# 44 slots of the first tile's expert mixer moved among the attention heads of the last tiles

## The reference

```python
def peer(h, w_pq, keys, u_tab, v_tab):
    ...
        q = (hb @ w_pq).reshape(t, P_HEADS, 2, P_QDIM // 2)
        sc = jnp.einsum('thpd,hpkd->thpk', q, keys).astype(jnp.float32)
        sv, si = lax.top_k(sc, P_TOPK)
        ...
        cv, ci = lax.top_k(cand, P_TOPK)
        eidx = jnp.take_along_axis(cidx, ci, axis=-1)
        gate = jax.nn.softmax(cv, axis=-1)
        act = jax.nn.gelu(jnp.einsum('thkd,td->thk', u_tab[eidx], hb).astype(jnp.float32))
        return jnp.einsum('thk,thkd->td', (gate * act).astype(hb.dtype), v_tab[eidx])
```

## Time and profile before

| | us |
|---|---|
| median of 3 runs | 5101.31 (5096.21 to 5101.77) |
| the profiled execution: its own time | 5101.03 |
| its span, first to last instruction | 5099.2 |
| PE busy | 3987.9 (78%) |
| DVE busy | 2904.9 (57%) |
| ACT busy | 1637.7 (32%) |
| DMA moved | 1577.22 MB, mean 309 GB/s |

### The profile page before, as it was taken

The page is one execution under the profiler, slowest core; times in us unless marked ns, Lnnn a source line. Parts: engine busy times, 40 slices in busy tenths (PEclk is TensorE's granted clock), DMA queues, the critical chain, the costliest instruction groups (busy, mean ns, idle before and its releaser), DMA issues.

```text
span 5099.2 us, 61250 instructions
## 1 busy us (share of the span) xinstructions
PE 3987.9 (78%) x19854; PEld 1568.1 (31%) x19854; DVE 2904.9 (57%) x6339; ACT 1637.7 (32%) x4803; POOL 1522.9 (30%) x1453
## 2 busy tenths in 40 slices
PE   5989988998886666666679899889988756666666
PEld 3555564232321111111134556633323211111111
DVE  3541464666787666554445414546667876665544
ACT  0222143333333333333322211433333333333333
POOL 0210002333444444333312100023333344443332
PEclk7989999999986777666679899999998867677666
DMA  7113305999999999999951133069999999999998
GB/s 280 48 51 124 132 26 210 408 413 383 421 415 393 421 421 421 421 421 421 421 195 48 51 128 136 18 239 407 411 396 421 394 399 421 421 421 421 421 421 355
DMA packets 223883, 1577.22 MB, mean 309 GB/s; under 512 B 25744, under 2 KB 27984, under 8 KB 35920
## 3 DMA queue, kind: packets, MB, share of 16 engines
q0 software_dynamic: 184320, 1342.26, 63.9%
q1 hardware_dynamic: 39248, 231.06, 12.1%
HBM read 1569.94 MB, written 3.28 MB: 309 GB/s over the span
## 4 chain that ended last, share of the span: by engine, by line
PE 40%; DMA 35%; DVE 16%; issue 4%; ACT 3%; DVEq 2%; SPq 0%; POOL 0%; ACTq 0%; POOLq 0%
DMA arena<-in_experts,arena 28%; PE ps L759 14%; PE ps L993 8%; DVE sq L1471 7%; DMA front<-in_experts,arena 6%; PE ps L944 4%; PE ps L969 3%; PE ps L896 2%; PE ps L957 2%; PE ps L921 2%; PE ps L908 1%; DMA arena<-in_weights 1%; DVE negm L1365 1%; DVE arena L1197 1%; PE ps L825 1%
## 5 line engine op out<-in xcount | busy, mean ns | idle before, releaser
L993 PE MATMUL ps<-arena 64*64 64x512 f32 x9088 | 1645.1, 810 | 834.4 <-ACT arena L1134 788.3
L732 POOL DMA_INDIRECT arena<-in_experts,arena x1136 | 1228.6, 1081 | 2824.6 <-PE ps L993 1738.0
L1471 DVE CUSTOM_DVE_ANT_0 sq<-arena 128x1024 f32<-128x1024 f32 x1136 | 1393.2, 1226 | 990.2 <-DMA arena<-in_experts,arena 926.5
L993 PEld LDWEIGHTS ps<-arena 64*64 64x64 f32 x9088 | 326.3, 162 | 2040.9 <-issue 2012.8
L1128 ACT ACTIVATE arena<-arena 128x1 f32<-128x1 f32 x1280 | 259.2, 203 | 1978.7 <-DVE arena L1471 1977.9
L759 PE MATMUL ps<-arena 128*128 128x512 f32 (+3 forms) x1920 | 787.7, 558 | 1.9 <-ACT arena L1042 0.9
L1134 ACT ACTIVATE arena<-ident,arena 128x128 f32<-128x128 f32 x1280 | 513.9, 401 | 91.6 <-issue 3.3
L759 PEld LDWEIGHTS ps<-arena 128*128 128x128 f32 x1920 | 353.2, 190 | 416.1 <-issue 377.7
L1130 ACT ACTIVATE arena<-arena 128x1 f32<-128x1 f32 x1280 | 376.8, 294 | 92.4 <-issue 5.6
L969 PE MATMUL ps<-arena 128*128 128x256 f32 (+1 forms) x1024 | 331.3, 466 | 3.1 <-issue 2.3
L993 PE MATMUL ps<-front,arena 64*64 64x512 f32 x1152 | 200.1, 770 | 90.2 <-ACT arena L1134 90.1
(11 more groups left out here) (158 smaller groups left out, 3005.7 us busy)
## 6 DMA issues: line engine op xcount, KB each, us to landing
arena<-in_weights SPq DMA_DIRECT2D x182, 1024.0 KB, 7.4
arena<-in_experts,arena POOLq DMA_INDIRECT x1136, 21.5
arena<-mod_rows SPq DMA_DIRECT2D x30, 512.0 KB, 6.9
arena<-in_weights SPq DMA_DIRECT2D x8, 576.0 KB, 4.6
arena<-in_keysT SPq DMA_DIRECT2D x4, 1024.0 KB, 9.8
arena<-in_weights SPq DMA_DIRECT2D x4, 768.0 KB, 4.2
arena<-in_weights SPq DMA_DIRECT2D x6, 512.0 KB, 3.5
front<-in_experts,arena POOLq DMA_INDIRECT x144, 15.2
```

What stands on the lines that cost most here:

```text
L732: pool.indirect_dma_start(out=ring[BUF[n]], out_offset=None, in_=ins["experts"], in_offset=bass.IndirectOffsetOnAxis(ap=index(t)[:, slot:s ...
L993: last = MM(acc[h][to:to + 64, c * 512:(c + 1) * 512], diag[n % 4][lo:lo + 64, lo:lo + 64], ring[BUF[n]][lo:lo + 64, D + c * 512:D + (c + ...
L1471: V.tensor_tensor_reduce(out=sq[:], in0=ring[BUF[n]][:, 0:D], in1=h2_of_slot(n), scale=1.0, scalar=0.0, op0=ALU.mult, op1=ALU.add, accum_o ...
```

## The change

Slots 0 to 43 of tile 0 (`FRONT` = 44) stand among the last 28 heads of tiles 2 to 4 in place of behind them, in both layers. To make room:

- all 26 items of `choose(l, 0)` stand among the first 20 heads (`mixed`), not among 48;
- the front slots use four buffers in turn: 4, and the new 11, 12 and 13. Buffer 11 is a gap gained by moving `va(0)`, `vc(0)` and others; 12 and 13 are two of the three weight blocks, so the loads that filled them early (`gate` half 2 and `proj` of the merge of tiles 2 to 4) wait for slots 42 and 43 (`HELD`);
- `acc[h]` is one bank (0 or 1), in which the two column halves lie on different partitions. `O` of tiles 2 to 4 moves to banks 2 and 3; while such a row of heads is open, pair (2,3) is not given out, and the other items choose among what is left;
- slots 0 to 47 compute gelu from Square, Identity and Tanh with the gate halved: six ACT instructions in place of three, so that no table is exchanged for each exp;
- merge and route of tiles 2 to 4 stand between slots 44 and 248.

```diff
+def mixed(items, more):
+    per, given, s = len(more) / len(items), 0, []
...
 def schedule():
...
-        s += attention(l, (2, 3, 4), choose(l, 0)) + [("rows2", l, 1), ("keys", l, 1), ("g2", l, 0)]
+        heads = attention(l, (2, 3, 4))
+        bare = heads.index(("s", l, 3, 0, 4))
+        s += mixed(heads[:bare], choose(l, 0))
         line = Line()
         line.slots(l)
-        line.spread(8, 100, choose(l, 1))
-        line.spread(-3, 248, pieces(merge(l, 1) + route(l, 1, 2)))
+        line.spread(-1, FRONT - 3, heads[bare:])
+        line.put(FRONT - 2.9, [("rows2", l, 1), ("keys", l, 1), ("g2", l, 0)])
+        line.spread(FRONT + 6, 116, choose(l, 1))
+        line.spread(FRONT, 248, pieces(merge(l, 1) + route(l, 1, 2)))
...
+    elif _k == "om":
+        _rows.discard(2 + _it[3])
     elif _k == "O":
         if _it[4] == 1:
-            _take(_it, _it[3], 1)
+            _b = _it[3] + 2 * (_it[2] > 1)
+            _take(_it, _b, 1)
+            _rows |= {_b} - {0, 1}
     elif _k in PAIR:
-        _take(_it, min((4, 6) if _open else (2, 4, 6), key=lambda b: max(_used[b:b + 2])), 2)
+        _take(_it, min((b for b in (2, 4, 6) if not _rows & {b, b + 1}), key=lambda b: max(_used[b:b + 2])), 2)
...
-    _there = [b for b in range(NBUF) if b not in RELEASE or (_s >= 6 and PLACE[RELEASE[b](_l)] < PLACE[("Emm", _n - 6)])]
+    _there = [4, 11, 12, 13] if _s < FRONT else [b for b in range(11) if b not in RELEASE or (_s >= 6 and PLACE[RELEASE[b](_l)] < PLACE[("Emm", _n - 6)])]
...
+                if n in HELD:
+                    sp.wait_ge(slot_used, HELD[n] + 1)
...
                         if t == 0 and slot == 0:
 
+                            pool.wait_ge(*ready("sink", l, 1))
+                            pool.wait_ge(*full("pq", l, 0, 15))
+                        if t == 0 and slot == FRONT:
+
                             pool.wait_ge(*ready("om", l, NT - 1, 1))
...
-                            last = MM(acc[h][to:to + 64, c * 512:(c + 1) * 512], diag[n % 4][lo:lo + 64, lo:lo + 64],
-                                      ring[BUF[n]][lo:lo + 64, D + c * 512:D + (c + 1) * 512], start=s == 0, stop=s == SLOTS - 1)
+                            last = MM(acc[h][to:to + 64, :], diag(n)[lo:lo + 64, lo:lo + 64],
+                                      row_in(n)[lo:lo + 64, D + c * 512:D + (c + 1) * 512], start=s == 0, stop=s == SLOTS - 1)
...
+                    if by_tanh(n):
+                        A(of(cube), of(dots), ACT.Square, scale=GELU_B ** 0.5)
+                        A(of(share), of(dots), ACT.Copy, scale=g)
+                        act.drain()
+                        A(of(inner), of(cube), ACT.Identity, scale=of(dots), bias=of(dots))
+                        act.drain()
+                        A(of(gel), of(inner), ACT.Tanh, scale=GELU_A)
+                        act.drain()
+                        A(of(wts), of(gel), ACT.Identity, scale=of(share), bias=of(share))
```

More of the change, by code:

```diff
@@ L36 @@
 NG = _at
+GELU_A = 0.7978845608028654
+GELU_B = 0.044715
 UNIT = 2048
@@ L270, with by_tanh @@
 LAG = 1.6
+FRONT = 44
+TANHS = FRONT + 4
+def mixed(items, more):
+    per, given, s = len(more) / len(items), 0, []
+    for i, it in enumerate(items):
+        s.append(it)
+        n = int(per * (i + 1) + 1e-6)
+        s += more[given:n]
+        given = n
+    return s + more[given:]
+def by_tanh(n):
+    return n % (NT * SLOTS) < TANHS
 def schedule():
@@ L310 @@
 _open = False
+_rows = set()
 def _take(it, bank, n):
@@ L449 @@
 FINAL_IN = {(l, b): max(n for n in range(NSLOT) if BUF[n] == b and ETILES[n // SLOTS][0] == l) for l in range(L) for b in range(NBUF)}
+LENT, HELD = [], {}
+for _l in range(L):
+    _k = LOAD_NO[_l, 1, ("gate", 0, 0)]
+    assert LOADS[_k + 1:_k + 3] == [(_l, 1, ("gate", 0, 1)), (_l, 1, ("proj", 0, 0))]
+    LENT.append(SPACE[_k + 1:_k + 3])
+    for _j in range(2):
+        HELD[_k + 1 + _j] = max(n for n in range(NSLOT) if BUF[n] == 12 + _j and ETILES[n // SLOTS] == (_l, 0))
 for _e, (_l, _t) in enumerate(ETILES):
@@ L533, in build @@
         cross = at(20480, D)
-        diag = [at(21504 + P * r, P) for r in range(4)]
+        diag = lambda n: at(21504 + P * (n % 4), P) if n % (NT * SLOTS) >= FRONT else ar(HT0 + D + P * (n % 4), P)
         index = lambda t: zt(t)[:, 1536:1664].bitcast(U32)
@@ L557, in build @@
         esum = take(8)
-        dots, gel, wts = (take(16) for _ in range(3))
+        dots, gel, wts, cube, inner, share = (take(16) for _ in range(6))
         assert _e[0] <= HT0 + D
         ps = ctx.enter_context(nc.psum_tensor("ps", [P, 8, 512], F32))
-        acc = [ps[:, 2 * h:2 * h + 2, :].rearrange("p a n -> p (a n)") for h in range(2)]
+        acc = [ps[:, h, :] for h in range(2)]
         fps = ps[:, :, :].rearrange("p a n -> p (a n)")
@@ L663, in _ @@
                     sp.wait_ge(*ready("om", l, (1, NT - 1)[c], 1))
+                    if c:
+                        sp.wait_ge(slot_used, max(n for n in range(NSLOT) if BUF[n] == 11 and ETILES[n // SLOTS][0] == l) + 1)
                     for copy, who in ((2, 1),) if c else ((0, 0), (1, 1)):
@@ L1121, in _ @@
                         act.wait_ge(*full("sw", *ETILES[e - 1]))
-                    A(cross[0:64, 0:512], acc[1][0:64, 512:D], ACT.Copy)
-                    out(A(cross[64:128, 0:512], acc[0][64:128, 512:D], ACT.Copy))
+                    A(cross[0:64, 0:512], acc[1][0:64, :], ACT.Copy)
+                    out(A(cross[64:128, 0:512], acc[0][64:128, :], ACT.Copy))
                 elif kind == "Ea":
@@ L1127, in _ @@
                     act.wait_ge(dot_done, n + 1)
-                    A(gel[:, c:c + 1], dots[:, c:c + 1], ACT.Gelu_apprx_tanh)
-                    act.drain()
-                    A(wts[:, c:c + 1], gel[:, c:c + 1], ACT.Copy, scale=gate(n // SLOTS % NT)[:, s:s + 1])
+                    of = lambda b: b[:, c:c + 1]
+                    g = gate(n // SLOTS % NT)[:, s:s + 1]
+                    if by_tanh(n):
[7 more added lines that the diff above has]
+                        A(of(wts), of(gel), ACT.Identity, scale=of(share), bias=of(share))
+                    else:
+                        A(of(gel), of(dots), ACT.Gelu_apprx_tanh)
+                        act.drain()
+                        A(of(wts), of(gel), ACT.Copy, scale=g)
                     act.drain()
@@ L1133, in _ @@
                         act.wait_ge(slot_used, n - 3)
-                    A(diag[n % 4], ident[:], ACT.Copy, scale=wts[:, c:c + 1]).then_inc(diag_done, 1)
+                    A(diag(n), ident[:], ACT.Copy, scale=wts[:, c:c + 1]).then_inc(diag_done, 1)
         @block.vector
@@ L1465, in _ @@
                     dve.drain()
-                    done(TT(g3, g3, esum.unsqueeze(2).to_broadcast([P, H, TOPK]), ALU.mult))
+                    last = TT(g3, g3, esum.unsqueeze(2).to_broadcast([P, H, TOPK]), ALU.mult)
+                    if t == 0:
+                        dve.drain()
+                        last = TS(gate(t)[:, 0:TANHS], gate(t)[:, 0:TANHS], 0.5, None, ALU.mult)
+                    done(last)
                     dve.drain()
```

33 lines of the change are left out of this document (18 added, 15 removed).

## The result

The changed kernel took 5169.68 us (median of 4 runs, 5167.12 to 5173.46), the one before 5101.54 beside it: ratio 1.0135, 95% interval 1.0122 to 1.0148. That is slower by 68 us, where the prediction's sum had 23.

A forecast was written before the change was run, and what follows sets the result against it. PE was taken to bound attention and merge, the DMA the route onward. Per layer 59 + 18 + 8 - 24.5 - 45 - 4 = 11.5 us lost, 23 in all: 5123 us, own range 5090 to 5150, wide range 5040 to 5175.

The forecast's parts named there:

- The first 20 heads: Start of tiles 2 to 4's attention: denser choices and two pairs of banks lose 18 us a layer, bounds 4 and 25.
- the last 28 heads: Rest of that attention, now with 41 slots among the heads: 59 us a layer lost, bounds 36 and 81.
- the merge: Merge of tiles 2 to 4: 24 slots fewer at PE's 1.02 us each, 24.5 us a layer saved.
- the route: DMA-bound stretch after the merge: 20 slots fewer, 45 us a layer saved, bounds 30 and 50.
- The friction term: Among the 48 heads: lower clock (0.88) and waits for four buffers add 8 us a layer, bounds 0 and 22.
- the walk: Last 28 heads: PE, DVE and ACT queues followed in order, giving 5.5 us a head against 3.5 before.
- The ACT part: ACT's six instructions for each front slot: 1.7 to 2.0 us, taken as 2.0, where it took 1.03.
- The rival with the DMA's price: Merge and route: each slot moved saves 2.49 us throughout, 110 us in place of 69.5; 5042 us, chance 0.1.
- The start gap: Last `om` to first Emm: gap stays, held loads land in it; 4 us saved, bounds 10 saved and 8 lost.
- The ring of four: Last 28 heads: the four gather buffers bind, 81 us lost in place of 59; 5167 us, chance 0.18.
- The collision in a bank: Slots' Emm: column halves sharing a bank could double its time; 5445 us, chance 0.02.
- Better interleaving: Last 28 heads: under 4.9 us a head; floor 5024 us, something between floor and forecast about 5060, chance 0.25.

The follow-up runs named there:

- c1: Kernel before with only tile 0's 26 choices moved among the first 20 heads, banks as before and no slots moved: 5114.67 us.
- a1: Changed kernel with `O` of tile 2 back in banks 0 and 1, so three pairs of banks go round through tile 2: 5107.39 us.
- c2: Kernel before with only the banks changed: sums in banks 0 and 1, `O` of tiles 2 to 4 in 2 and 3: 5248.08 us.
- c5: c2 with one more 256-column matmul, its result unread, in front of each `s` of tiles 2 to 4: 5215.0 us.
- c3: Kernel before with both the choices among the first 20 heads and the bank part, no slots moved: 5271.25 us.
- a2: Changed kernel with three ACT instructions in place of six for the first 48 slots, part of the gelu left out: 5131.65 us.
- v4: a1 with tiles 3 and 4's `O` in bank 2, one-bank items in bank 3, three front-slot gelu steps on DVE instead of ACT: 5086.14 us.
- c4: Kernel before with only the sums in one bank each, `O` staying in banks 0 and 1, three pairs going round: 5102.74 us.

## Why the prediction was right and wrong

**The first 20 heads: the term that failed.** It was 18 us and measured 42, in each layer. Twice 24 is 48 us, and the whole miss is 45 (68 against 23); the other errors nearly cancel: the last 28 heads took as much as forecast with their friction, the merge gave 9 us a layer more and the route 7 less. The step is "1.66 + 0.96 + 0.90 + 0.2 of handover = 3.7 us a head": it costs the loop of two pairs with durations that were read at a clock of 0.95 and more, and leaves `O` out of it. By that price and the 3.3 for m = 1 the 20 heads come to 71 us, 6 more than before, and the choices to the other 12. In the changed kernel the clock there was 0.73, `s` took up to 2.93 us and `O` 2.83, and `O`'s own wait of up to 2.95 held up the next `s`. c1 and a1 show that 13 to 18 us belong to the choices, a little more than the 12, and a1 and c2 that 24 to 33 belong to the pairs, in place of 6. c5 shows that part of those is the clock. The friction term knew of a lower clock, but put it at 0.88 by the rows of another stage, and its 8 us for all 48 heads was too little. (The 16 us of friction in the prediction's last part are not what its sum has; the heads grew by 108 us, against 85 in the sum.)

**The last 28 heads: the size right by luck, the reason half right.** Forecast 59 and a share of friction, measured 66.3 and 66.8. But the walk puts the loss on the turn-taking with the slots, and c2 loses 42 to 44 there without any slot. More than half of what the walk had put on the slots comes with the pairs alone, so it is luck that the sum is right. The slots themselves add 33 and 24 us over c3, 0.7 each in the mean, which is less than their 1.02 on PE: they fill PE's waits, and the clock is 0.94 and 0.93 where c3's is 0.84 and 0.76. The ACT part was priced right. By form, in that stretch:

```profile
L1199 ACT ACTIVATE arena<-ident,arena 128x128 f32<-128x128 f32 x41 | 16.5, 401 | 2.8
L1191 ACT ACTIVATE arena<-arena 128x1 f32<-128x1 f32 x41 | 15.9, 387 | 3.3 <-issue 0.6
L1187 ACT ACTIVATE arena<-arena 128x1 f32<-128x1 f32 x41 | 15.9, 387 | 3.1 <-issue 0.3
L1185 ACT ACTIVATE arena<-arena 128x1 f32<-128x1 f32 x41 | 11.7, 284 | 0.0
...
L1189 ACT ACTIVATE arena<-arena 128x1 f32<-128x1 f32 x41 | 8.3, 203 | 2.8
```

Identity with two operands per partition takes 0.387 us, just past the upper end of 0.29 to 0.38, and the six instructions with their drains about 2.0. By the Trainium skill (ScalarE: Activation LUTs, section What ACT_TABLE_LOAD costs) each such operand adds about 93 ns; the steps here, 196 to 203 with none, 284 to 294 with one and 387 with two, bear it out. That this length matters is shown by a2 (-16 and -15 us) and v4.

**The merge: mechanism right, gain larger.** Emm's busy time in start gap and merge, before (L993):

```profile
820.50:1267.00 446.50, 157.33 (x1120) 30.92 (x1120) 0.95 0.99 396
```

and with every engine's work, before:

```profile
820.50:1267.00 446.50, 411.09 (x1698) 127.56 (x1696) 268.37 (x506) 144.83 (x450) 170.05 (x147) 0.95 0.99 396
```

After, Emm's own row:

```profile
929.70:1337.00 407.30, 131.16 (x952) 25.81 (x952) 0.99 0.97 382
```

26.2 us less, for 21 slots fewer in this cut (1.12 and 1.10 us each): PE's price, not the DMA's 2.49. The rival with the DMA's price had the merge shorter by 60, and it is 34 to 40, so the rival falls; but the DMA share stayed at 0.97, where the prediction had it near 0.9. Of the further 13.6 us, 8.4 are PE idling less (446.5 - 411.1 = 35.4, and 407.3 - 380.3 = 27.0), and 5 are its other work, at a clock of 0.99 in place of 0.95. That is read from the rows, and no run isolates it. The start gap has the Emm of the last front slots at 933.0, 4.1 us behind the last `om`, and the second `gate` half, which was held back for slot 42, is waited for 1.27 us at 946 (timeline above): cheap, as forecast.

**The route: right.** -38.7 and -36.6, forecast -45 with bounds 30 and 50; 20 slots fewer gave 1.9 us each, and not 2.25. The rest of the layer did not move.

**The other rivals.** The ring of four did not bind. The landings between 790 and 900 us, where the DMA is not full:

```profile
arena<-in_experts,arena POOLq DMA_INDIRECT x21, 5.6
```

The median is 5.6 us, at the low end of the earlier trace rows, and not 9.1. And the dot products hardly wait for their gathers among the last 28 heads (769 to 929 us):

```profile
DVE sq L1540 <- DMA arena<-in_experts,arena: 6.1, 6, 2.2
DVE sq L1540 <- DMA front<-in_experts,arena: 2.1, 2, 1.1
```

This rival's price of 5167 is nearly the time measured, by another mechanism: a right number is no proof of a story. It is also what stretched the wide range to 5175, so that the time lies in it is luck; it is outside the forecast's own 5090 to 5150. The collision in a bank is ruled out by c4. Better interleaving needed under 4.9 us a head over the last 28; it was 5.7, and 5.1 even in v4.

The two conditions under which the prediction called itself wrong (last 28 heads under 145 us, merge shorter by 60) did not come about. Both looked at the side where the time would have been better than forecast; neither watched the first 20 heads.

## What to carry to other kernels

A PSUM bank taken from a loop is not a detail of the layout. Write down which engine waits for whom once the buffers go round one fewer, with every instruction that stands in the in-order queue, and price those on the waiting loop at the clock of a PE that idles, not at that of the busy profile. Work from elsewhere is cheap in such a loop as long as it fills waits that are there (0.7 us a slot here in the mean, where merge and route gave back 1.7; the first 22 slots next to nothing, the second 22 some 1.25 each), and its price doubled from 44 slots to 56. When a change clears room and then uses it, measure the clearing alone: here it cost 170 us (c3), the use gave back 102, and a looser rule for the tile that needed no clearing recovered 62.

## What the runs showed of the hardware that was not expected

- Adding matmuls made the program faster: c5 does 96 matmuls more than c2 and takes 33 us less, while the granted clock goes from 0.78 and 0.77 to 0.94 and 0.99 in the two stretches of layer 0. A loop in which PE waits for DVE and ACT is thus slower twice, by its waits and by the clock that they bring.
- The same four score matmuls took 1.56 us at 691 us of the changed kernel and 2.93 at 766, in one attention, at a granted clock of 0.96 and 0.50 (1.2 GHz); a duration of a matmul is only a number beside its clock.
- Two 64-row column halves accumulated in one bank, by Emm after Emm of 128 slots a tile, cost as much as in two banks: 5102.74 against 5101.41 us.
